# A decoder layer's feed-forward: a first tile pair of plain products, another order on GpSimd, another product order, and four token tiles at the end

## The chip, the cores and the metric

One core of one Trainium2 chip runs the whole kernel. The metric is the device time of one execution in microseconds (us). The engines are TensorE (PE in the profile, with its weight loads as PEld), VectorE (DVE), ScalarE (ACT), GpSimd (POOL) and SyncE (SP), which issues nearly all the DMAs.

## What is computed

The layer has an RWKV-7 group and an attention group, whose outputs are mixed, added to the input and normalised. A feed-forward follows. The change touches only what comes after the mix product, in float32:

```python
x = layer_norm(ALPHA * x + mix, ln1_g[l], ln1_b[l])
f = jnp.square(jax.nn.relu(x @ w_ffn1[l])) @ w_ffn2[l]
x = layer_norm(ALPHA * x + f, ln2_g[l], ln2_b[l])
```

There are 1024 tokens, a model width of 1024 and a hidden width of 4096.

## The kernel before, in words

**Precision.** Each float32 operand is split into a high part (a copy to the format fp32r, mostly by ScalarE) and a low part (VectorE or GpSimd subtracts). Each product is three matmuls, high by high, high by low, and low by high. In all these products the moving operand has 512 columns; a transpose is a matmul with 128.

**Seven products for eight.** Both feed-forward products are cut into 2x2 blocks and done by a Strassen-Winograd scheme with seven block products, p1 to p7, instead of eight. A block product of the first half is 4 contraction tiles (`HK`) of 3 matmuls, 12 in all, and leaves one 128x512 bank. The scheme needs sums of the weight blocks (s1 to s4, GpSimd, function `sums`), sums of the token blocks (`b12_raw`, `t3_raw` and the t tiles, made once by VectorE and GpSimd), and sums of the results (VectorE, `added`).

**First half (FFN1).** The 4096 hidden rows are 32 tiles, taken as 16 pairs u = 0 to 15 (`NU`): tiles u and u+16. For each pair TensorE does seven products, so 84 matmuls. ScalarE and VectorE split the weight pieces of the next pair (`w_high`, `w_low`); GpSimd sums its weight blocks (`sums(u + 1)`) and forms four sums of the hidden tiles of the present pair (`hidden_sums(u)`), which the second half needs. VectorE combines the seven results (`added`) and applies relu and square (`squared`). SyncE writes seven tiles of each pair to DRAM (`spill`) and loads the weights two pairs ahead into one landing buffer (`load1`). All engines run the lists written here in program order and meet at semaphores.

In program order GpSimd does, for each pair, `sums(u+1)` and then `hidden_sums(u)`; `hidden_sums(0)` comes before the loop. On VectorE `w_low(nxt, 2)` stands between the p6 and p7 results, and p5's result waits until the sums of the pair before are made.

**The first pair (u = 0)** runs while the first normalisation ends. Its p1 and p2 use tokens 0 to 511 (`LO`), which are normalised and transposed early. Its other products need tokens 512 to 1023 (`HI`): TensorE transposes them (`turn_high`), and for each contraction tile ScalarE, VectorE and GpSimd form and split the token sums. There are two buffers each of `b12_raw` and `t3_raw`, and one bank each for B12 and B22.

**Second half (FFN2).** There are 56 steps q = 8 i + p: product i of seven, contraction pair p of eight. A step has 24 matmuls (2 contraction tiles, 4 token tiles, 3 terms). It needs a pair of hidden tiles from DRAM and a piece of `w_ffn2`, 512 KB each, loaded by `load2(q)` into one of six stages (`RING`), and split by `high2` and `low2`. For the products listed in `COMBINED` GpSimd subtracts a 128x1024 weight piece first (`combine`). When a product's eight steps are done, VectorE reads its four banks (`read`), and GpSimd adds kept parts (`add`); both stand three steps later in their engine's list (`LAG = 3`). The last four steps are run token tile by token tile. Each of the eight token tiles has statistics (`part_stats`, `aggregate`), and a `finish` of two 128x1024 operations on VectorE, then a DMA.

```python
for u in range(1, NU):
    if u < NU - 1:
        sums(u + 1)
    hidden_sums(u)
```

Of the kernel before, what the change touches and what calls it, by code (L numbers as in the profile page):

```python
# [24 lines left out]
P = 128  # L25
# [1913 lines left out]
def mix_ffn(nc, mem, k, t, out):  # L1939
# [28 lines left out]
    b12_raw = [mem.at(f"b12_raw{j}", 70 + 4 * j, [P, HALF]) for j in range(2)]  # L1968
    t3_raw = [mem.at(f"t3_raw{j}", 72 + 4 * j, [P, HALF]) for j in range(2)]
# [41 lines left out]
    first_set = pieces("0", (A12_, quarters(190, 0), 198, 190), (S12_, None, 178, 202),  # L2011
                       (("s3", "a22"), quarters(190, 1), 174, 194), (("s4",), None, 182, 4))
    second_set = pieces("1", (A12_, quarters(46, 0), 42, 38), (("s1",), None, 62, 188),
                        (("s2", "s4"), quarters(46, 0), 54, 46), (("s3", "a22"), quarters(46, 1), 58, 50))
# [6 lines left out]
    def raw_of(u, name):  # L2021
# [9 lines left out]
           for i, n in enumerate(("h11", "h12", "h21", "h22", "s1", "s2", "s3", "s4"))}  # L2031
    ORDER = ("p1", "p5", "p6", "p7", "p3", "p2", "p4")
    order = lambda u: {0: ("p1", "p2", "p3", "p7", "p5", "p6", "p4"),
                       1: ("p1", "p2", "p5", "p6", "p7", "p3", "p4")}.get(u, ORDER)
    FIRST_BANK = {"p1": 0, "p2": 0, "p3": 4, "p4": 1, "p5": 2, "p6": 3, "p7": 5}
    BANKS = (6, 7, 3, 5, 2, 4, 0, 1)
    READ = {"p1": 1, "p6": 1, "p7": 2, "p5": 4, "p3": 5, "p2": 6, "p4": 7}
    nth = lambda u, name: 7 * (u - 1) + order(u).index(name)
    bank_of = lambda u, name: FIRST_BANK[name] if u == 0 else BANKS[nth(u, name) % 8]
    B12_BANK, B22_BANK = 6, 7  # L2040
# [26 lines left out]
    PAIR_BANK = ((2, 4), (6, 0))  # L2067
    banks = lambda b, n: ps[:, b:b + n, :]

    with ExitStack() as ctx:  # L2070
# [25 lines left out]
        def _(sp):  # L2096
# [44 lines left out]
            sp.wait_ge(sums_w, 8)  # L2141
            for n in (1, 3):
                sp.wait_ge(t_split[n][1], T_ALL)
            sp.wait_ge(t2_made, T_ALL)
            for u in range(NU):
                if u < NU - 2:
                    if u:
                        sp.wait_ge(lo_w, 4 * (u + 1) + 2)
                        sp.wait_ge(sums_w, 4 * (u + 2))
                    load1(u + 2)  # L2150
                elif u == NU - 1:
                    sp.wait_ge(prod, 7 * (NU - 1))
                    sp.wait_ge(lo_w, 4 * NU)
                    sp.wait_ge(sums_w, 4 * NU)
# [28 lines left out]
        def _(pe):  # L2183
# [22 lines left out]
            def turn_high(kt):  # L2206
                if kt:
                    pe.wait_ge(b12_copied, kt)
                turn(B12_BANK, 4, kt).then_inc(b12_ready, 1)
                if kt:  # L2210
                    pe.wait_ge(b22_lo, kt)
                turn(B22_BANK, 4, HK + kt).then_inc(b22_ready, 1)
# [13 lines left out]
            def whole(u, name):  # L2226
                i, _ = wset(u)[1][STILL[name]]
                pe.wait_ge(lo_w, 4 * u + i + 1)
# [28 lines left out]
            turn_high(0)  # L2257
            pe.wait_ge(lo_w, 4)
# [579 lines left out]
```

## Time and profile before

| | us |
|---|---|
| median of 3 runs | 1521.74 |
| lowest and highest run | 1521.64, 1525.98 |
| the profiled execution: its own time | 1523.78 |
| the profiled execution: its span | 1522.0 |
| TensorE busy | 1406.6 (92%) |
| VectorE busy | 918.1 (60%) |
| ScalarE busy | 450.6 (30%) |
| GpSimd busy | 447.2 (29%) |
| mean granted TensorE clock | 0.961 |

A span runs from the first to the last instruction of one execution. The granted clock is a share of TensorE's full speed of 2.4 GHz, so 0.5 is 1.2 GHz. Busy times of matmuls are modelled and overlap, so stretches are better compared by the distance between starts than by busy time. A row's square bracket gives the idle time before it and what ended it.

### The profile page before, as it was taken

Reading aid. Unit: us, or ns where it says so; the run is one execution under the profiler, and the core shown is the slowest. Engines: PE = TensorE matmul, PEld = TensorE weight load, DVE = VectorE, ACT = ScalarE, POOL = GpSimd, SP = SyncE. Lnnn points to the kernel's source line nnn. Section 1 sums busy time; section 2 is a strip of 40 time slices with the busy share of each in tenths; the row PEclk is TensorE's granted clock in tenths of the full one; section 3 lists DMA queues with packets and bytes.
Section 4 is the critical chain, followed back from the end, with each engine's and each line's share of the span. In section 5 each row is a group of like instructions: output and inputs, shape, how many; then the busy total and the mean of one; then the engine's idle time right before and its main releaser. Section 6 shows DMA issues by size and latency. Waiting matters only on the chain. (4 is left out here: it accounts for less than half of the span.)

```text
span 1522.0 us, 24832 instructions
## 1 busy us (share of the span) xinstructions
PE 1406.6 (92%) x10596; PEld 1149.6 (76%) x10596; DVE 918.1 (60%) x1020; ACT 450.6 (30%) x614; POOL 447.2 (29%) x291
## 2 busy tenths in 40 slices
PE   6999999888999799999699699999998799999995
PEld 5878888666777599996588488777777588888874
DVE  3547654263655244436747977766665675757768
ACT  2134433133344333322103412222111344433320
POOL 0000223200242200000137565555564154411450
PEclk8999999989999899999899799999999899999998
DMA  5111244578358921111413134433434787555642
GB/s 199 42 56 50 90 147 145 151 158 234 87 152 252 222 66 44 44 25 56 171 65 110 42 125 153 147 143 127 150 145 152 269 276 249 193 193 194 194 138 111
DMA packets 144686, 211.80 MB, mean 139 GB/s; under 512 B 79456, under 2 KB 82144, under 8 KB 143936
## 3 DMA queue, kind: packets, MB, share of 16 engines
q1 hardware_dynamic: 144384, 209.69, 43.1%
q8 instruction: 84, 1.38, 0.4%
q10 hardware_dynamic: 192, 0.52, 0.1%
q14 instruction: 26, 0.21, 0.0%
HBM read 136.18 MB, written 64.29 MB: 132 GB/s over the span
## 5 line engine op out<-in xcount | busy, mean ns | idle before, releaser
L2288 PE MATMUL banks<-stage_b_hi,stage_a_hi 128*128 128x512 f32 x448 | 177.5, 396 | 18.9 <-DVE stage_b_lo L2520 11.9
L2288 PE MATMUL banks<-stage_b_lo,stage_a_hi 128*128 128x512 f32 x448 | 176.8, 395 | 0.0
L2288 PE MATMUL banks<-stage_b_hi,stage_a_lo 128*128 128x512 f32 x448 | 176.6, 394 | 0.0
L2517 DVE TENSOR_TENSOR stage_a_lo<-stage_a_raw,stage_a_hi 128x1024 fp32r<-128x1024 f32 x56 | 98.2, 1754 | 72.0 <-ACT stage_a_hi L2376 71.9
L2288 PEld LDWEIGHTS banks<-stage_b_hi,stage_a_hi 128*128 128x128 f32 x448 | 85.7, 191 | 39.0 <-DVE stage_b_lo L2520 13.6
L358 PE MATMUL banks<-xT_hi,win_hi 128*128 128x512 f32 x320 | 103.6, 406 | 4.6 <-DVE xT_lo L705 4.6
L358 PE MATMUL banks<-xT_lo,win_hi 128*128 128x512 f32 x320 | 100.4, 395 | 0.0
L358 PE MATMUL banks<-xT_hi,win_lo 128*128 128x512 f32 x320 | 100.1, 395 | 0.0
L2288 PEld LDWEIGHTS banks<-stage_b_lo,stage_a_hi 128*128 128x128 f32 x448 | 85.7, 191 | 18.0
L2288 PEld LDWEIGHTS banks<-stage_b_hi,stage_a_lo 128*128 128x128 f32 x448 | 85.5, 191 | 17.9
L2376 ACT ACTIVATE stage_a_hi<-stage_a_raw 128x1024 fp32r<-128x1024 f32 x56 | 59.3, 1058 | 132.5 <-DMA stage_b_raw<-in_w_ffn 108.2
L2683 POOL TENSOR_TENSOR tile_s<-tile_h,tile_h 128x512 f32<-128x512 f32 x32 | 41.4, 1294 | 142.9 <-DVE tile_h L2498 142.9
L1140 PE MATMUL banks<-probs,v_all 128*128 128x512 f32 (+3 forms) x192 | 75.0, 504 | 0.7 <-ACT probs L1235 0.7
L358 PEld LDWEIGHTS banks<-xT_hi,win_hi 128*128 128x128 f32 x320 | 60.8, 193 | 19.1 <-DVE xT_lo L705 4.8
L1301 DVE TENSOR_REDUCE row_max_parts<-banks 128x1 f32<-128x512 f32 (+1 forms) x96 | 50.1, 552 | 35.7 <-PE banks L1092 24.0
L358 PEld LDWEIGHTS banks<-xT_lo,win_hi 128*128 128x128 f32 x320 | 61.3, 191 | 13.2
L358 PEld LDWEIGHTS banks<-xT_hi,win_lo 128*128 128x128 f32 x320 | 61.2, 191 | 13.0
L1235 ACT ACTIVATE probs<-banks 128x1024 f32<-128x1024 f32 (+3 forms) x64 | 41.6, 651 | 88.7 <-PE banks L1125 51.4
L2498 DVE SCALAR_TENSOR_TENSOR tile_h<-tile_h 128x512 f32<-128x512 f32 x64 | 63.1, 986 | 1.7
L2702 POOL TENSOR_TENSOR w_slots<-stage_b_raw,w_slots 128x1024 f32<-128x1024 f32 x16 | 41.8, 2611 | 65.0 <-DMA stage_b_raw<-in_w_ffn 65.0
L747 POOL COPY norm_wide<-key_norm 128x1024 f32<-128x1024 f32 x4 | 5.1, 1264 | 186.5 <-DVE cum_tile L666 186.5
L1363 POOL TENSOR_TENSOR att_out<-att_v,att_sum 128x512 f32<-128x512 f32 x7 | 8.9, 1271 | 168.2 <-DVE att_sum L1315 139.6
(375 smaller groups left out, 3626.2 us busy)
## 6 DMA issues: line engine op xcount, KB each, us to landing
stage_b_raw<-in_w_ffn SPq DMA_DIRECT2D x50, 512.0 KB, 4.6
w_landed<-in_w_ffn SPq DMA_DIRECT2D x32, 512.0 KB, 4.4
hid_s<-tile_s SPq DMA_DIRECT2D x64, 256.0 KB, 2.0
stage_a_raw<-hid_s SPq DMA_DIRECT2D x32, 512.0 KB, 3.7
hid_h<-tile_h SPq DMA_DIRECT2D x48, 256.0 KB, 2.0
stage_a_raw<-hid_h SPq DMA_DIRECT2D x24, 512.0 KB, 3.7
win_raw<-in_w_in SPq DMA_DIRECT2D x20, 512.0 KB, 3.6
x_tok<-in_x SPq DMA_DIRECT2D x8, 512.0 KB, 7.4
```

Source lines behind the costliest of these rows:

```text
L358: last = mm(ps[:, 2 * j + b, :], w[j][:, kt, :], r[:, kt, b * HALF:(b + 1) * HALF], start=kt == 0 and i == 0, stop=kt == KT - 1 and i == 2)
L747: G.tensor_copy(out, src).then_inc(wide_done, 1)
L1140: last = mm(ps[:, O[b], lo - b * HALF:HALF], pair[:, 64 * (h % 2):64 * (h % 2) + P], probs[kt % 3][:, lo:(b + 1) * HALF], start=kt == 0, s ...
L1235: A_(probs[kt % 3][:, kt * P:S], flat(T[kt % 2])[:, kt * P:S], ACT.Exp, scale=SCALE)\
L1301: V.reduce_max(tops[:, n, qt:qt + 1], ps[:, b, 0:width], AX_X).then_inc(a_free[b], 1)
L1363: G.tensor_tensor(k.att_out[:], k.att_v[:], k.att_sum[:], ALU.mult).then_inc(y_ready, 1)
L2288: last = nc.tensor.matmul(ps[:, bank, :], s[a][:, j, tok], s[b][:, j, :], start=p == 0 and j == 0 and n == 0, stop=p == NP - 1 and j == 1 ...
L2376: A(s["a_hi"][:], s["a_raw"][:], COPY).then_inc(hi2, 1)
L2498: V.scalar_tensor_tensor(hid[name][:], hid[name][:], 0.0, hid[name][:], ALU.max, ALU.mult).then_inc(hid_done, 1)
L2517: V.tensor_tensor(s["a_lo"][:], s["a_raw"][:], s["a_hi"][:].bitcast(F32), ALU.subtract).then_inc(lo2, 1)
L2683: G.tensor_tensor(dst, a, b, op).then_inc(sums_h, 1)
L2702: G.tensor_tensor(dst, a, b, ALU.subtract).then_inc(combined, 1)
```

## The change

It has five parts.

1. **Pair 0** isn't done with seven products. Its four result tiles (h11, h21, h12, h22) are plain products of 8 contraction tiles by 3 matmuls, 96 matmuls, the two for tokens 0 to 511 first. ScalarE applies relu and VectorE the square. No weight sums are needed for it (`sums(0)` goes), only its two pieces of weights. The token sums aren't needed for it either: they now stand beside the plain products and beside pair 1, in whole buffers (`b12_raw`, `t3_raw` of four tiles) and with two banks each for the transposes. Pair 1 takes the order p1, p2, p3, p7, p5, p6, p4.
2. **GpSimd** does `sums(u + 1)` and then `hidden_sums(u - 1)`: the hidden sums stand one pair later. `sums(u)` waits for pair u-2, as before.
3. **VectorE and SyncE in FFN1**: `w_low(nxt, 3)` stands before p5. In the last pair the splits of steps 0 and 1 of FFN2 stand after p5 and after p2 instead of at the head; `load2(2)` and `load2(3)` are issued inside the last pair, and the last spills of pair 14 no longer stand ahead of pair 15's.
4. **FFN2's product order**: the one combined product among the last three (h22) comes fifth (i = 4) instead of seventh, and the last (h21) isn't combined. The token tiles 4 to 7 are complete after the fifth product. So their statistics and `finish` stand at steps 44 to 49, and only token tiles 0 to 3 are left for the end.
5. **The reads**: `read(3)` has two more 128x1024 operations (the base of tiles 0 to 3), `read(4)` is now a plain addition for tiles 4 to 7, and `add(4)` of GpSimd goes; its four additions stand in `add(5)`.

The core of the diff ("..." marks what is left out):

```diff
-    A_OF = ("h11", "s1", "s2", "s3", "s4", "h21", "h22")
-    B_OF = ((0, 0), (0, 1), (1, 1), (0, 0), (1, 1), (1, 0), (1, 0))
-    COMBINED = (1, 2, 3, 6)
+    A_OF = ("h11", "s1", "s2", "s3", "h22", "s4", "h21")
+    B_OF = ((0, 0), (0, 1), (1, 1), (0, 0), (1, 0), (1, 1), (1, 0))
+    COMBINED = (1, 2, 3, 4)
...
-    PAIR_BANK = ((2, 4), (6, 0))
+    STATS_AT = (44, 45, 46, 47)
+    LAST_TILES = (4, 5, 6, 7, 0, 1, 2, 3)
+    PAIR_BANK = ((6, 0), (2, 4))
...
+            sp.wait_ge(sums_w, 4)
+            sp.wait_ge(t_split[1][1], T_ALL)
+            load1(2)
+            spill(0, ("h22", hid_done, 1), ("h11", hid_done, 3), ("h21", hid_done, 4))
+            for u in range(1, NU):
...
+                    sp.wait_ge(lo_w, split_base(u + 1) + 2)
+                    sp.wait_ge(sums_w, 4 * (u + 1))
                     load1(u + 2)
...
+                if u == NU - 1:
+                    sp.wait_ge(prod, 7 * (NU - 2))
+                    sp.wait_ge(lo_w, split_base(NU))
+                    sp.wait_ge(sums_w, 4 * (NU - 1))
                     load2(0)
                     load2(1)
-                spill(u)
-            sp.wait_ge(prod, 7 * NU)
-            for q in range(2, STEPS):
+                    sp.wait_ge(prod, prods(u, "p5"))
+                    load2(2)
+                spill(u - 1, *SUMS)
...
+                if u == NU - 1:
+                    sp.wait_ge(prod, prods(u, "p2"))
+                    load2(3)
+                spill(u, ("h21", hid_done, 4))
+            spill(NU - 1, *SUMS)
+            sp.wait_ge(prod, 7 * (NU - 1))
+            for q in range(4, STEPS):
...
+            pe.wait_ge(lo_w, 2)
+            pe.wait_ge(xlow_hi, HK + 2)
+            for part in range(2):
+                pe.wait_ge(xlow_lo, HK * (part + 1))
+                for i in range(2):
+                    for kt in range(HK * part, HK * (part + 1)):
+                        last = first(i, kt, x_hi[:, kt, LO], x_lo[:, kt, LO], i)
+                    if part:
+                        last.then_inc(first_mm, 1)
...
+            for kt in range(2):
+                turn_high(kt)
+            for kt in range(HK):
+                pe.wait_ge(b12_lo, kt + 1)
+                pe.wait_ge(b22_lo, kt + 1)
+                for i in range(2):
+                    for n, part in enumerate((kt, HK + kt)):
...
+                if kt + 2 < HK:
+                    turn_high(kt + 2)
...
             second_half(0)
+            second_half(1)
+            first_part(0)
+            first_part(1)
+            second_half(2)
+            second_half(3)
             for kt in range(HK):
                 high_t(3, kt)
-                if kt < HK - 1:
-                    second_half(kt + 1)
-                for n in (1, 2, 4):
-                    high_t(n, kt)
             act.wait_ge(x1_out, 16 * TT)
-            act.wait_ge(sums_w, 8)
+            act.wait_ge(sums_w, 4)
             for i in (1, 2, 3):
                 w_high(1, i)
+            for kt in range(HK):
+                high_t(1, kt)
+                high_t(2, kt)
+            first_part(2)
+            first_part(3)
+            for kt in range(HK):
+                high_t(4, kt)
...
+                    for q in range(4):
+                        high2(q)
...
+                dve.wait_ge(b12_hi, kt + 1)
+                V.tensor_tensor(t_lo[4][:, kt, :], b12_raw[:, kt, :], t_hi[4][:, kt, :].bitcast(F32), ALU.subtract)\
+                    .then_inc(b12_lo, 1)
                 dve.wait_ge(b22_hi, kt + 1)
-                V.tensor_tensor(t3_raw[kt % 2][:], ps[:, B22_BANK, :], b12_raw[kt % 2][:], ALU.subtract).then_inc(t3_made, 1)
-                V.tensor_tensor(x_lo[:, HK + kt, HI], ps[:, B22_BANK, :], x_hi[:, HK + kt, HI].bitcast(F32), ALU.subtract)\
+                V.tensor_tensor(x_lo[:, HK + kt, HI], ps[:, b22_bank(kt), :], x_hi[:, HK + kt, HI].bitcast(F32), ALU.subtract)\
                     .then_inc(b22_lo, 1)
+                V.tensor_tensor(t3_raw[:, kt, :], ps[:, b22_bank(kt), :], b12_raw[:, kt, :], ALU.subtract).then_inc(t3_made, 1)
...
+                second_half(kt)
             for i in (1, 2, 3):
                 w_low(1, i)
+            for kt in range(HK):
+                for n in (3, 1, 2):
+                    low_t(n, kt)
+            dve.wait_ge(first_mm, 4)
+            for kt in range(HK):
+                low_t(4, kt)
...
-                if 0 < u < NU - 1:
+                if nxt < NU:
                     w_low(nxt, 0)
                     w_low(nxt, 1)
-                elif u:
-                    low2(0, 0)
...
-                if 0 < u < NU - 1:
+                if nxt < NU:
                     w_low(nxt, 2)
                 settle(u, 1)
                 added(u, "p7", u3_sb[:], u2_sb[:])
+                if nxt < NU:
+                    w_low(nxt, 3)
                 settle(u, 2)
                 dve.wait_ge(sums_h, 4 * u)
-                left(u, "h22")
...
-                if 0 < u < NU - 1:
-                    w_low(nxt, 3)
-                elif u:
-                    low2(1, 0)
-                    low2(1, 1)
+                if nxt == NU:
+                    low2(0, 0)
+                    low2(0, 1)
...
+                if nxt == NU:
+                    low2(1, 0)
+                    low2(1, 1)
...
+                    for h in range(2):
+                        at = xo[:, 2 * h:2 * h + 2, LO]
+                        V.scalar_tensor_tensor(at, at, ALPHA, p1_all[:, 2 * h:2 * h + 2, :], ALU.mult, ALU.add).then_inc(based, 1)
+                elif i == 4:
+                    dve.wait_ge(based, 6)
+                    for h in range(2):
+                        at = xo[:, 4 + 2 * h:6 + 2 * h, LO]
+                        V.tensor_tensor(at, banks(bank[h], 2), at, ALU.add).then_inc(read2, 1)
...
+                if q in STATS_AT:
+                    tt = LAST_TILES[STATS_AT.index(q)]
...
+                    dve.wait_ge(read2, 6)
+                    part_stats(tt, 0)
+                    part_stats(tt, 1)
+                    aggregate(tt)
+                if q - 2 in STATS_AT:
+                    finish(LAST_TILES[STATS_AT.index(q - 2)], (slice(0, D),))
+            dve.wait_ge(added2, 6)
+            for tt in range(4):
...
+                dve.wait_ge(out_mm, tt + 1)
+                step.mark(V.tensor_tensor(xo[:, tt, LO], ps[:, PAIR_BANK[0][tt // 2] + tt % 2, :], xo[:, tt, LO], ALU.add))
...
-            sums(0)
...
+            for kt in range(HK):
                 pool.wait_ge(t2_made, kt + 1)
-                G.tensor_tensor(b21, b21, b11, ALU.subtract).then_inc(t4_made, 1)
+                G.tensor_tensor(xt_raw[:, HK + kt, :], xt_raw[:, HK + kt, :], xt_raw[:, kt, :], ALU.subtract).then_inc(t4_made, 1)
...
-            hidden_sums(0)
             for u in range(1, NU):
                 if u < NU - 1:
                     sums(u + 1)
-                hidden_sums(u)
+                hidden_sums(u - 1)
+            hidden_sums(NU - 1)
...
-                dst, a, b = {1: (at, s, at), 2: (at, s, at), 3: (s, at, s), 6: (s, s, at)}[i]
+                dst, a, b = {1: (at, s, at), 2: (at, s, at), 3: (s, at, s), 4: (s, s, at)}[i]
...
-                first, cut, kept, ready = {
-                    3: (4, HI, (p5_all,), (based, 0)), 4: (0, HI, (u2_all, p5_all), (read2, 4)), 5: (0, LO, (p1_all,), (read2, 6))}[i]
+                first, kept, ready = {3: (4, (p5_all,), (based, 0)), 5: (0, (u2_all, p5_all), (read2, 6))}[i]
...
-                if (q - LAG) % NP == NP - 1 and 3 <= (q - LAG) // NP < 6:
+                if (q - LAG) % NP == NP - 1 and (q - LAG) // NP in (3, 5):
```

## Rows read from the trace of the kernel before

**Rows 1.** windows; columns: stretch, its us, then busy us of each engine (instructions), PEclk, DMA
```profile
832.90:876.90 44.00, 30.47 (x117) 22.92 (x116) 40.51 (x42) 20.43 (x33) 23.46 (x16) 0.77 0.19 70
876.90:1175.90 299.00, 288.42 (x1261) 235.47 (x1259) 207.26 (x218) 58.65 (x70) 169.38 (x116) 1.00 0.39 142
1175.90:1211.30 35.40, 21.66 (x74) 17.01 (x74) 22.30 (x23) 12.51 (x13) 5.39 (x4) 0.81 0.68 254
1211.30:1477.70 266.40, 266.40 (x1177) 220.60 (x1176) 179.28 (x110) 105.24 (x103) 108.81 (x40) 1.00 0.65 214
1477.70:1507.30 29.60, 24.46 (x97) 18.77 (x96) 28.43 (x40) 2.83 (x7) 0.28 (x1) 0.94 0.22 87
1507.30:1522.00 14.70, 0.01 (x1) 0.00 (x0) 11.25 (x17) 0.59 (x2) 0.00 (x0) 0.66 0.28 112
```

**Rows 2.** timeline of the SP queue; columns: start, duration, instruction
```profile
1194.07 0.38 SPq L2120 DMA_DIRECT2D stage_a_raw<-hid_h  x1
...
1456.19 0.33 SPq L2120 DMA_DIRECT2D stage_a_raw<-hid_h  x1
...
1461.63 0.33 SPq L2120 DMA_DIRECT2D stage_a_raw<-hid_h  x1
```

**Rows 3.** timeline of TensorE before and in pair 0 (L2197 transposes)
```profile
825.80 1.80 PE L2197 MATMUL banks<-ident,x 128*128 128x128 f32 x15
...
862.66 0.80 PE L2222 MATMUL banks<-x1T_hi,w_hi 128*128 128x512 f32 x1 [4.47 <-DVE x1T_lo L2477]
```

**Rows 4.** timeline of all engines around pair 15's start (brackets: idle time before)
```profile
1151.13 1.74 POOL L2645 TENSOR_TENSOR wo_raw<-w_landed 128x512 f32<-128x512 f32 x1
...
1157.00 2.00 ACT L2319 ACTIVATE wo_hi<-wo_raw 128x1024 fp32r<-128x1024 f32 x2 [11.30 <-POOL wo_raw L2653]
...
1159.46 0.47 PE L2222 MATMUL banks<-x1T_hi,wo_hi 128*128 128x512 f32 x1 [1.07 <-DVE wo_lo L2424]
...
1164.38 1.29 POOL L2683 TENSOR_TENSOR tile_s<-tile_h,tile_h 128x512 f32<-128x512 f32 x1 [7.42 <-DVE tile_h L2498]
```

**Rows 5.** timeline of all engines, end of pair 15
```profile
1176.89 1.06 ACT L2376 ACTIVATE stage_a_hi<-stage_a_raw 128x1024 fp32r<-128x1024 f32 x1 [17.89 <-DMA stage_b_raw<-in_w_ffn]
...
1180.26 0.68 DVE L2503 TENSOR_TENSOR u_sb<-banks,p_sb 128x512 f32<-128x512 f32 x1
...
1183.05 0.79 PE L2288 MATMUL banks<-stage_b_hi,stage_a_hi 128*128 128x512 f32 x1 [6.98 <-DVE tile_h L2503]
```

**Rows 6.** waits of TensorE, 1184 to 1507 us: total, times, longest
```profile
PE banks L2288 <- DVE stage_b_lo L2520: 11.9, 4, 6.8
```

**Rows 7.** timeline of VectorE in and after pair 0
```profile
840.20 1.28 DVE L2467 SCALAR_TENSOR_TENSOR x<-x,ln_sd,ln_bias 128x1024 f32<-128x1024 f32 x1
...
855.06 0.68 DVE L2477 TENSOR_TENSOR x1T_lo<-banks,x1T_hi 128x512 fp32r<-128x512 f32 x1
...
857.37 3.43 DVE L2484 TENSOR_TENSOR t_lo<-x1T_raw,t_hi 128x512 fp32r<-128x512 f32 x2
...
868.40 1.28 DVE L2484 TENSOR_TENSOR t_lo<-x1T_raw,t_hi 128x512 fp32r<-128x512 f32 x2
...
882.93 4.01 DVE L2424 TENSOR_TENSOR we_lo<-w_landed,we_hi 128x1024 fp32r<-128x1024 f32 x2
```

**Rows 8.** timeline of VectorE in FFN2
```profile
1369.15 2.35 DVE L2575 TENSOR_TENSOR u_all<-banks,u_all 128x1024 f32<-128x1024 f32 x2 [7.99 <-PE banks L2288]
1371.61 9.03 DVE L2581 SCALAR_TENSOR_TENSOR x_out<-x_out,u_all 128x1024 f32<-128x1024 f32 x4
...
1420.72 3.41 DVE L2517 TENSOR_TENSOR stage_a_lo<-stage_a_raw,stage_a_hi 128x1024 fp32r<-128x1024 f32 x1
```

**Rows 9.** timeline of GpSimd in FFN2
```profile
1372.92 6.64 POOL L2713 TENSOR_TENSOR x_out<-x_out,p_all 128x1024 f32<-128x1024 f32 x2 [28.67 <-DVE x_out L2581]
```

**Rows 10.** timeline of VectorE at the end
```profile
1509.89 0.68 DVE L2628 TENSOR_TENSOR x_out<-banks,x_out 128x512 f32<-128x512 f32 x1
...
1514.49 0.69 DVE L2628 TENSOR_TENSOR x_out<-banks,x_out 128x512 f32<-128x512 f32 x1
```

More of the change, by code:

```diff
@@ L1967, in mix_ffn @@
     xt_raw = mem.at("x1T_raw", 78, [P, KT, HALF])
-    b12_raw = [mem.at(f"b12_raw{j}", 70 + 4 * j, [P, HALF]) for j in range(2)]
-    t3_raw = [mem.at(f"t3_raw{j}", 72 + 4 * j, [P, HALF]) for j in range(2)]
+    b12_raw = mem.at("b12_raw", 70, [P, HK, HALF])
+    t3_raw = mem.at("t3_raw", 150, [P, HK, HALF])
     t_hi = {n: mem.at(f"t{n}_hi", 126 + 16 * (n - 2), [P, HK, HALF], F32R) for n in (2, 3, 4)}
@@ L2206, in turn_high, with first @@
             def turn_high(kt):
[L2207 to L2212, printed above, removed]
+                if kt >= 2:
+                    pe.wait_ge(b12_hi, kt - 1)
+                    pe.wait_ge(t3_made, kt - 1)
+                turn(b12_bank(kt), 4, kt).then_inc(b12_ready, 1)
+                turn(b22_bank(kt), 4, HK + kt).then_inc(b22_ready, 1)
+            def first(i, kt, b_hi, b_lo, bank):
+                made, _ = first_set
+                _, a_hi, a_lo = made[i]
+                j, cut = kt // HK, slice(kt % HK * P, (kt % HK + 1) * P)
+                for n, (a, b) in enumerate(((a_hi, b_hi), (a_hi, b_lo), (a_lo, b_hi))):
+                    last = nc.tensor.matmul(ps[:, bank, :], a[:, j, cut], b, start=kt == 0 and n == 0,
+                                            stop=kt == KT - 1 and n == 2)
+                return last
             def one(u, name, kt):
@@ L2256, in _ @@
             pe.wait_ge(last_normed, 1)
-            turn_high(0)
-            pe.wait_ge(lo_w, 4)
-            for name, ready in (("p3", b22_lo), ("p7", t_split[3][1]), ("p5", t_split[1][1]), ("p6", t_split[2][1]),
-                                ("p4", t_split[4][1])):
-                for kt in range(HK):
-                    if name == "p3" and kt < HK - 1:
-                        turn_high(kt + 1)
-                    pe.wait_ge(ready, kt + 1)
-                    last = one(0, name, kt)
-                last.then_inc(prod, 1)
+            for kt in range(2):
[5 more added lines that the diff above has]
+                    for n, part in enumerate((kt, HK + kt)):
+                        b_hi, b_lo = (t_hi[4][:, kt, :], t_lo[4][:, kt, :]) if n == 0 else (x_hi[:, part, HI], x_lo[:, part, HI])
+                        made, _ = first_set
+                        _, a_hi, a_lo = made[i]
+                        cut = slice(kt * P, (kt + 1) * P)
+                        for m, (a, b) in enumerate(((a_hi, b_hi), (a_hi, b_lo), (a_lo, b_hi))):
+                            last = nc.tensor.matmul(ps[:, 2 + i, :], a[:, n, cut], b, start=kt == 0 and n == 0 and m == 0,
+                                                    stop=kt == HK - 1 and n == 1 and m == 2)
+                    if kt == HK - 1:
+                        last.then_inc(first_mm, 1)
+                if kt + 2 < HK:
+                    turn_high(kt + 2)
+            BUILT = {"p7": t_split[3][1], "p5": t_split[1][1], "p6": t_split[2][1], "p4": t_split[4][1]}
             for u in range(1, NU):
@@ L2405, in keep @@
                     A(dst[:, 2 * h:2 * h + 2, :], banks(PAIR_BANK[i][h], 2), COPY).then_inc(copied2, 1)
-            for q in range(2, STEPS):
+            roots = 0
+            for q in range(4, STEPS):
                 high2(q)
@@ L2410, in _ @@
                     keep((q - LAG) // NP)
[L2411 to L2413 removed]
+                if q - 1 in STATS_AT:
+                    root2(LAST_TILES[roots])
+                    roots += 1
+            for tt in LAST_TILES[4:]:
+                root2(tt)
         @block.vector
```

215 lines of the change are left out of this document (88 added, 127 removed).

## Prediction

> **What bounds the kernel now.** I read four views in this order: the windows by stage, the waits of TensorE, the timelines where TensorE stands still, and the timelines of the engines it waits for. The reader is to see that TensorE is the bound from 832.9 us on, but with gaps, and that after its last matmul 14.7 us follow without it [rows 1]. The stages before 832.9 us are left alone.
>
> A step of FFN2 takes 1461.63 - 1456.19 = 5.44 us when nothing is late [rows 2]. That is 24 matmuls, so 0.2267 us each. With this price the stages of [rows 1] come apart:
>
> - Pair 0 takes 44.0 us. Its 84 matmuls are worth 19.0 us and its 32 transposes, at 1.80/15 = 0.12 us [rows 3], 3.8 us. The rest is waiting for token sums, one gap of 4.47 us among it, at the lower clock level in part (granted clock 0.77).
> - Pairs 1 to 15 take 299.0 us, and 15 x 84 matmuls are worth 285.6 us. The missing 13.4 us are a bubble of about 1.3 us at the p5 product of each later pair, until VectorE has split the sums of weights [rows 4]. What sets it is a loop: GpSimd's weight sums start at 1151.13, ScalarE begins to split them at 1157.00, VectorE follows and only then takes p7 and p5, and after these GpSimd gets its hidden tiles at 1164.38, with the next weight sums behind them [rows 4].
> - FFN2, from 1175.9 to 1507.3, takes 331.4 us, and 56 steps are worth 304.6 us. Of the missing 26.8 us, 7.0 [rows 5] and 11.9 [rows 6] are idle. The other 7.9 us are matmuls at the lower clock level (1.2 GHz) after the gaps of 7.0, 6.8 and 3.4 us (granted clock 0.81 and 0.94 in [rows 1]): some 2.5 us for each long gap.
>
> **Pair 0.** It gets 96 matmuls, 21.8 us, and keeps 32 transposes, 3.8 us. The first 48 matmuls need only tokens 0 to 511 and last 10.9 us, to 843.8; the last normalisation ended at 840.20 + 1.28 [rows 7], so it is hidden. Then 16 transposes. The first B22 tile is ready after three copies of ScalarE (about 0.5 us each, half of one of 128x1024 in [rows 4]) and two operations of VectorE from PSUM of 0.68 us [rows 7], some 1.1 us after the transposes. Later tiles are hidden behind 12 matmuls each, but for about 0.4 us. Sum: 21.8 + 3.8 + 1.5 = 27.1 us, a gain of **16.9**. Bounds: 25.6 without waits, 31 if the clock falls at this gap. I take it not to fall, as the bubbles of 1.07 us [rows 4] leave the clock at 1.00 [rows 1].
>
> **Pairs 1 and 2.** Pair 1 starts at 860.0 and asks for p7 after three products, at 868.2. For that VectorE must have split the third sum of all four tiles. Its list: last `t3_raw` at about 858.2, then three weight splits, then 12 `low_t` of which the tenth is the one wanted. GpSimd meanwhile makes six sums, to about 868.5. With GpSimd at work a VectorE subtraction of 128x512 takes 3.43/2 = 1.7 us and one of 128x1024 takes 4.01/2 = 2.0 us; alone the small one takes 0.64 us [rows 7]. So 2.0 + 2.0 + 3 x 1.7 brings it to 867.3 to 868.5 with two `low_t` done, and eight more take 4.8 us: 873.3. TensorE waits 5.1 us, and 2.5 us for the clock. Pair 2 starts at 860.0 + 19.0 + 7.6 = 886.6.
>
> Pair 2's p6 goes to the bank of pair 1's p2, so it waits for VectorE to have taken that. The chain: ten more operations of VectorE (two `low_t`, four of t4, four squares) to 879.3; `sums(2)`, which now waits for these squares, 5.9 us (1151.13 to 1157.00 [rows 4]) and some 0.8 of contention, to 886.0; `hidden_sums(0)`, four of 1.29 us [rows 4] with waits of their own, 6.2 us, to 892.2; VectorE's wait for these stands ahead of p5, and six operations of 0.68 us end with p2 at 896.3. TensorE is there at 892.0: 4.3 us and 2.5 us for the clock, 6.8 us. Bounds for both stalls together: 8 us if VectorE is never held up by GpSimd (then only the second chain is late), 20 us if every step is contended. I take 7.6 + 6.8 = 14.4.
>
> **Pairs 3 to 15.** `sums(u + 1)` can start when pair u starts and ends at +5.9; the splits are done by about +13, and the next pair wants them at +19. `hidden_sums(u - 1)` ends at +12.1, when VectorE has just taken p7 and split its weights. So the loop is gone, and a pair is 84 matmuls, 19.04 us. The queue behind VectorE's wait for the hidden sums is p5, p3, p2, p4; the next pair asks for the p5 bank only at +24.5. `load1` and the spills move in SP's queue: a load is issued at +6 and has 13 us. FFN1 after pair 0: 285.6 + 14.4 = 300.0 us against 299.0, a loss of **1.0**: the bubbles pay for the two stalls.
>
> **Into FFN2.** Before, the splits of step 0 stood ahead of pair 15's results in VectorE's list and their load ended at 1176.89, so the p6 result was taken at 1180.26 and TensorE waited 6.98 us for a bank [rows 5]. Step 2 was loaded at 1194.07 [rows 2], after all spills. Now the splits stand behind p5 and p2, at +13 and +18 of the pair, with the load ended at about +7; `load2(2)` goes out at +6 and `load2(3)` at +18, and step 2 is wanted at +30. Both gaps go. If this cover failed, each would cost its 7 us and 2.5 us again.
>
> **Step 35.** `read(3)` starts at step 32 and took 2.35 and then 9.03 us for four operations, two of them held up by GpSimd's two additions of 6.64 us [rows 8, 9]. One VectorE operation beside one of GpSimd costs about 3.35 us (3.41 in [rows 8]). It ended 11.6 us after the step's start; step 35 is wanted at 16.3. Now two more operations stand there, and then the two splits of step 35. And GpSimd, which had nothing to combine in the fifth product, now has `combine(35)` to `combine(38)` behind its additions. Taking turns, VectorE ends at 11.6 + 4 x 3.35 = 25.0. TensorE waits 8.7 us and loses 2.5 us by the clock: 11.2 us. The lower bound is nothing: alone such an operation takes (9.03 - 6.64)/2 = 1.2 us, and 11.6 + 4 x 1.2 = 16.4. I take the full price, since the rows show turns whenever both have work.
>
> **Last steps.** Statistics and finishes of four tiles (about 4 us each) move into steps 42 to 49: with splits of 2.35 us and the read that is 37 us of VectorE in 43.5 us, and it runs ahead (idle 7.99 us at step 32 [rows 8]). GpSimd's four additions now hold up the splits of steps 51 and 52 only; those of 53 to 55 end about 23 us after step 48 starts, and are wanted from 23.1 to 25.8. So the gaps behind 1477.7 go. FFN2: 304.6 + 11.2 = 315.8 us against 331.4, a gain of **15.6**.
>
> **End.** VectorE needs 4.6 us for a tile (1509.89 to 1514.49 [rows 10]), TensorE 5.44 us for its quarter of the last four steps. With nothing left from other tiles VectorE keeps up, and after the last matmul there remain 0.2 us and the 7.5 us from 1514.49 to the span's end: 7.7 against 14.7, a gain of **7.0**.
>
> **Sum.** 16.9 - 1.0 + 15.6 + 7.0 = 38.5 us off the span of 1522.0: 1483.5. The profiled execution took 1523.78 us itself, 2.0 above the median of the runs, 1521.74; taken off the median it gives 1483.2 us.
>
> **Rivals.**
>
> - *No wait at step 35.* If VectorE gets its operations through, TensorE never stops there: 1483.2 - 11.2 = 1472. For it speaks that it is a matter of 8.7 us in eight operations; against it the turns of [rows 8, 9]. Chance 0.25. The Trainium skill (SBUF — State Buffer, section "SBUF: two separate sides") has VectorE and GpSimd share one port pair under an exclusive lock held for a whole instruction by whoever starts first; it promises no turns, so VectorE could win several times running, and the time would be 1472; with turns it stays 1483. It exempts operations that read PSUM, and the 0.68 us one amid GpSimd's work [rows 7] agrees.
> - *The loop stays*, because something else in VectorE's list is late each pair: 13 pairs at 20.3 us cost 17 us more, 1500. Chance 0.08. Against it: 5 us to spare in each pair.
> - *The loads into FFN2 aren't hidden*: 9.5 to 19 us more, 1493 to 1502. Chance 0.07.
> - *Still fewer stalls* in pairs 1 and 2 beside none at step 35: under 1465. Chance 0.07.
> - *Slower than before.* The hidden sums come too late: VectorE can't free the p5 bank. It starts when GpSimd's eight sums end later than 24.5 - 1.4 = 23.1 us after the pair's start; slower overall needs 14 pairs at 19.04 + 38.5/14 = 21.8 us, so an end at 25.9 in place of 12.1. The longest sum in [rows 4] is 1.74 us, and eight of those are 13.9. Chance 0.03.
>
> **Chances and range.** The forecast has 0.5, by itself 1476 to 1491. To hold 8 in 10 the range takes in the first rival and the upper bounds of the stalls: 1465 to 1494. A difference under 0.3%, 4.6 us, can't be told from none: slower 0.03 (the last rival), same 0.03 (the loop and the loads going wrong together, with the full stalls), faster 0.94.
>
> **What would show it.** Pair 0 some 27 us long; one gap before p7 of pair 1 and one before p6 of pair 2; no bubbles from pair 3 on; no gap between the halves; a gap at step 35, with VectorE's operations of 3.3 us beside `combine`; no gaps in the last four steps, and 7.7 us after the last matmul. It would be wrong above all if contention of VectorE and GpSimd is milder or harsher than in these rows.

## Result, and the profile after

The changed kernel takes 1486.5 us (median of 4 runs, 1485.18 to 1489.19), the kernel before beside it 1521.93 us (1521.64 to 1525.98). The ratio is 0.976, 95% interval 0.974 to 0.979: 35.4 us less, where 38.5 were predicted. The profiled execution took 1487.25 us with a span of 1485.5.

First the windows of the changed kernel by stage, with the columns of [rows 1]: pair 0, pairs 1 and 2 up to the end of their stalls, the other pairs, FFN2, and what follows the last matmul.

```profile
832.90:860.20 27.30, 25.66 (x129) 21.16 (x128) 15.80 (x21) 12.30 (x22) 15.70 (x12) 1.00 0.18 73
860.20:906.00 45.80, 34.08 (x133) 27.04 (x133) 37.79 (x41) 16.31 (x26) 32.24 (x20) 0.85 0.29 104
906.00:1161.80 255.80, 255.80 (x1131) 211.87 (x1130) 191.50 (x204) 56.94 (x67) 169.61 (x103) 1.00 0.46 161
1161.80:1477.70 315.90, 307.40 (x1345) 253.87 (x1343) 239.44 (x173) 113.82 (x117) 114.09 (x41) 0.98 0.63 211
1477.70:1485.50 7.80, 0.22 (x1) 0.00 (x0) 4.57 (x8) 0.29 (x1) 0.00 (x0) 0.80 0.34 134
```

From 906.0 to 1161.8 TensorE is busy for 255.80 of 255.80 us: the bubble of each pair [rows 4] is gone. As long as TensorE has work, the granted clock is below 1.00 only in the two stretches with waits of over 5 us, pairs 1 and 2 and one place of FFN2. Next all waits of TensorE from 832 to 1490 us (total, times, longest).

```profile
PE banks L2321 <- DVE stage_b_lo L2564: 8.5, 1, 8.5
PE banks L2243 <- DVE tile_h L2551: 5.9, 1, 5.9
PE banks L2243 <- DVE t_lo L2531: 5.3, 1, 5.3
PE banks L2293 <- DVE x1T_lo L2521: 1.6, 2, 1.3
PE banks L2243 <- DVE we_lo L2472: 0.4, 1, 0.4
```

Six gaps are left. The timeline of TensorE says where (the matmul behind a gap, and of some its successors; the gap of 0.4 us, at p5 of pair 2, isn't shown).

```profile
843.63 1.91 PE L2209 MATMUL banks<-ident,x 128*128 128x128 f32 x16
846.82 0.47 PE L2293 MATMUL banks<-t_hi,w_hi 128*128 128x512 f32 x1 [1.28 <-DVE x1T_lo L2521]
847.13 0.39 PE L2293 MATMUL banks<-t_lo,w_hi 128*128 128x512 f32 x1
...
857.40 0.47 PE L2293 MATMUL banks<-t_hi,w_hi 128*128 128x512 f32 x1 [0.35 <-DVE x1T_lo L2521]
...
873.91 0.80 PE L2243 MATMUL banks<-t_hi,w_hi 128*128 128x512 f32 x1 [5.35 <-DVE t_lo L2531]
874.50 0.63 PE L2243 MATMUL banks<-t_lo,w_hi 128*128 128x512 f32 x1
874.93 0.63 PE L2243 MATMUL banks<-t_hi,w_lo 128*128 128x512 f32 x1
...
899.15 0.79 PE L2243 MATMUL banks<-t_hi,we_hi 128*128 128x512 f32 x1 [5.95 <-DVE tile_h L2551]
...
1360.81 0.80 PE L2321 MATMUL banks<-stage_b_hi,stage_a_hi 128*128 128x512 f32 x1 [8.50 <-DVE stage_b_lo L2564]
1361.40 0.63 PE L2321 MATMUL banks<-stage_b_lo,stage_a_hi 128*128 128x512 f32 x1
```

The gaps of 5 us and more stand before p7 of pair 1, p6 of pair 2 and step 35, as forecast. Behind them matmuls come 0.43 us apart (874.50 to 874.93), the lower clock level; behind the gap of 1.28 us they come 0.23 us apart once the first two have started, the upper one. FFN2's start follows from step 35: 1360.81 - 8.50 - 35 x 5.44 = 1161.9.

VectorE and, below it, GpSimd from step 32 on (compare [rows 8, 9]):

```profile
1336.03 2.36 DVE L2624 TENSOR_TENSOR u_all<-banks,u_all 128x1024 f32<-128x1024 f32 x2 [6.47 <-PE banks L2321]
1338.49 9.03 DVE L2630 SCALAR_TENSOR_TENSOR x_out<-x_out,u_all 128x1024 f32<-128x1024 f32 x4
1347.44 6.73 DVE L2633 SCALAR_TENSOR_TENSOR x_out<-x_out,p_all 128x1024 f32<-128x1024 f32 x2
1354.10 3.37 DVE L2561 TENSOR_TENSOR stage_a_lo<-stage_a_raw,stage_a_hi 128x1024 fp32r<-128x1024 f32 x1
1357.39 3.37 DVE L2564 TENSOR_TENSOR stage_b_lo<-stage_b_raw,stage_b_hi 128x1024 fp32r<-128x1024 f32 x1
...
1339.79 6.64 POOL L2768 TENSOR_TENSOR x_out<-x_out,p_all 128x1024 f32<-128x1024 f32 x2 [12.59 <-DVE x_out L2630]
1346.39 16.60 POOL L2758 TENSOR_TENSOR stage_b_raw<-stage_b_raw,w_slots 128x1024 f32<-128x1024 f32 x5
```

From 1347.44 VectorE's four operations take 6.73/2, 6.73/2, 3.37 and 3.37 us, and GpSimd's five take 16.60/5 = 3.32 us each: from here to GpSimd's last `combine` they take turns without an exception.

VectorE at the end (compare [rows 10]):

```profile
1461.63 0.69 DVE L2681 TENSOR_TENSOR x_out<-banks,x_out 128x512 f32<-128x512 f32 x1 [3.21 <-PE banks L2321]
...
1477.95 0.69 DVE L2681 TENSOR_TENSOR x_out<-banks,x_out 128x512 f32<-128x512 f32 x1 [0.75 <-PE banks L2321]
```

Here it is VectorE that waits for TensorE, 0.75 us at the last tile, and 7.55 us follow. Before, VectorE lagged: its last tile came 7.2 us after TensorE's end at 1507.3.

### The profile page after: what moved, and what is told of

Same layout as the page of the kernel before. It is cut to its first block, busy times and chain, and to the rows that moved or that the text cites. A ratio compares the mean times of both kernels' runs of the same rounds, so it can differ in the third digit from the quotient of the medians.

```text
span 1485.5 us, 24855 instructions
## 1 busy us (share of the span) xinstructions
PE 1393.8 (94%) x10608; PEld 1145.3 (77%) x10608; DVE 919.2 (62%) x1017; ACT 450.6 (30%) x619; POOL 466.2 (31%) x285
## 4 chain that ended last, share of the span: by engine, by line
PE 45%; DVE 3%; issue 1%; POOL 1%; DMA 0%; ACT 0%; SPq 0%; DVEq 0%; POOLq 0%
PE banks L2321 20%; PE banks L2243 18%; PE banks L2202 6%; PE banks L2231 1%; DVE x_out L2630 1%; DVE x_out L2633 0%; DMA w_landed<-in_w_ffn 0%; PE banks L2293 0%; PE banks L2209 0%; DVE t_lo L2531 0%; DVE stage_b_lo L2564 0%; DVE stage_a_lo L2561 0%; DVE x1T_lo L2531 0%; POOL tile_s L2739 0%; DVE u_all L2624 0%
## 5 line engine op out<-in xcount | busy, mean ns | idle before, releaser
L2561 DVE TENSOR_TENSOR stage_a_lo<-stage_a_raw,stage_a_hi 128x1024 fp32r<-128x1024 f32 x56 | 102.0, 1822 | 42.7 <-ACT stage_a_hi L2414 42.7
L1301 DVE TENSOR_REDUCE row_max_parts<-banks 128x1 f32<-128x512 f32 (+1 forms) x96 | 50.1, 551 | 35.4 <-PE banks L1092 23.6
L358 PEld LDWEIGHTS banks<-xT_lo,win_hi 128*128 128x128 f32 x320 | 61.2, 191 | 13.1
L1796 POOL TENSOR_TENSOR k_undecayed<-hT,undecay 128x256 f32<-128x256 f32 x16 | 11.8, 740 | 134.9 <-ACT undecay L1657 134.9
L2564 DVE TENSOR_TENSOR stage_b_lo<-stage_b_raw,stage_b_hi 128x1024 fp32r<-128x1024 f32 x34 | 51.2, 1507 | 0.4
```

What stands on the lines that cost most here:

```text
L358: last = mm(ps[:, 2 * j + b, :], w[j][:, kt, :], r[:, kt, b * HALF:(b + 1) * HALF], start=kt == 0 and i == 0, stop=kt == KT - 1 and i == 2)
L1301: V.reduce_max(tops[:, n, qt:qt + 1], ps[:, b, 0:width], AX_X).then_inc(a_free[b], 1)
L2561: V.tensor_tensor(s["a_lo"][:], s["a_raw"][:], s["a_hi"][:].bitcast(F32), ALU.subtract).then_inc(lo2, 1)
L2564: V.tensor_tensor(s["b_lo"][:], src, s["b_hi"][:].bitcast(F32), ALU.subtract).then_inc(lo2, 1)
```

## Experiments

All kernels are the changed one with one edit more, and all were timed beside the kernel before. The stages ahead of the feed-forward, which no edit touches, vary by some 5 us from one execution to the next (the first transpose of pair 0's second half starts at 841.6 to 846.9). And the kernel before took 1521.9 us beside the changed kernel, 1525.6 beside e1 to e4, 1524.6 beside e5 to e8 and 1524.5 beside e9 and e10, so medians of different rows can be compared to some 4 us only. So the traces are also compared **from that transpose to the span's end**: 1485.5 - 843.63 = 641.9 us in the changed kernel. The last column is this difference. It is from one execution each, and the clock behind a gap moves it by up to 1.5 us for each gap (last section).

| run | median, us | ratio to before (95%) | from the transpose, us | against the changed kernel |
|---|---|---|---|---|
| changed kernel | 1486.5 | 0.976 (0.974-0.979) | 641.9 | |
| e1_pool_old_order | 1502.2 | 0.985 (0.984-0.986) | 656.3 | +14.4 |
| e2_base_late | 1480.6 | 0.971 (0.969-0.973) | 634.9 | -7.0 |
| e3_add_late | 1477.7 | 0.969 (0.968-0.971) | 630.4 | -11.5 |
| e4_both_late | 1477.4 | 0.968 (0.967-0.970) | 630.9 | -11.0 |
| e5_t3_first | 1488.1 | 0.976 (0.974-0.977) | 641.4 | -0.5 |
| e6_loads_late | 1495.9 | 0.981 (0.979-0.983) | 650.7 | +8.8 |
| e7_finish_end | 1490.7 | 0.978 (0.976-0.980) | 646.1 | +4.2 |
| e8_fine_waits | 1483.8 | 0.973 (0.971-0.974) | 638.5 | -3.4 |
| e9_late_fine | 1473.7 | 0.967 (0.966-0.969) | 625.4 | -16.5 |
| e10_best | 1473.0 | 0.967 (0.964-0.969) | 625.3 | -16.6 |

**e1_pool_old_order: does GpSimd's order remove the bubbles?**

```diff
             for u in range(1, NU):
+                hidden_sums(u - 1)
                 if u < NU - 1:
                     sums(u + 1)
-                hidden_sums(u - 1)
```

GpSimd's sequence is then that of the kernel before.

> The changed kernel, but GpSimd does the hidden sums of pair u-1 ahead of the weight sums of pair u+1 again. Theory: the old loop is back, so TensorE shows a bubble of about 1.3 us at p5 of each of some 12 later pairs and a pair takes 20.3 us in place of 19.04; 15 to 17 us more, less up to 6 us because the wait of pair 2 is another one: a span of 1495 to 1503 us. Rival: the bubbles went because VectorE's third weight split stands ahead of p5 and because the loads of weights are issued elsewhere; then the span stays within 3 us of 1485.5.

The waits of TensorE in this run, and two neighbouring p5 products:

```profile
PE banks L2243 <- DVE we_lo L2472: 8.3, 6, 4.4
...
PE banks L2243 <- DVE wo_lo L2472: 4.5, 6, 0.8
```

```profile
1115.95 0.47 PE L2243 MATMUL banks<-x1T_hi,wo_hi 128*128 128x512 f32 x1 [0.75 <-DVE wo_lo L2472]
1136.18 0.47 PE L2243 MATMUL banks<-x1T_hi,we_hi 128*128 128x512 f32 x1 [0.76 <-DVE we_lo L2472]
```

The bubbles are back, and a pair takes 1136.18 - 1115.95 = 20.23 us in place of 19.04. The trace has eleven of them, in pairs 5 to 15, which make 13.1 us. FFN2's first steps lose 2.9 us besides (2.1 of it in waits), and pair 2 and step 35 cost some 1.5 us less (in pair 2 the wait of 5.95 us at p6 turns into one of 4.4 at p5). By the traces the run is 14.4 us longer; by the medians, each against the kernel before beside it, 12.1. So one moved call is worth a third to two fifths of the whole gain of 35.4. The bubble is the loop described in the prediction, and pair 0 has no part in it.

**e2, e3, e4: which work makes step 35 late?** VectorE's two operations on tiles 0 to 3 (the base) go from step 32 to step 40 in e2; GpSimd's additions go behind step 39 and step 50's `combine` in e3; e4 has both.

```diff
 # e2
-                    for h in range(2):
-                        at = xo[:, 2 * h:2 * h + 2, LO]
-                        V.scalar_tensor_tensor(at, at, ALPHA, ...)
...
+                if q == 40:
+                    (the same three lines)
 # e3
-                if (q - LAG) % NP == NP - 1 and (q - LAG) // NP in (3, 5):
-                    add((q - LAG) // NP)
+                if q in (39, 50):
+                    add({39: 3, 50: 5}[q])
```

> The changed kernel, but the two additional base operations of read(3) stand on VectorE after step 40's splits. Theory (turns with GpSimd, 3.35 us for each operation of VectorE while GpSimd has work): step 35 is ready 18.3 us after the start of step 32 in place of 25.0, so TensorE waits 2.0 us in place of 8.5 and its clock doesn't fall: 8.9 us less, a span near 1476.6. Rival (VectorE's own list is too long, GpSimd has no part in it): two operations at their own 1.2 us, 2.3 us less, 1483.

> The changed kernel, but GpSimd's two additions after the fourth product stand behind combine(39) instead of behind combine(34). VectorE's list is unchanged. Theory: GpSimd then has only combine(37) and combine(38) in this stretch, as their loads land, so two of VectorE's eight operations are held up and step 35 is ready about 16 us after the start of step 32, when it is wanted at 16.3: the gap of 8.5 us and the clock's 2.4 us go, a span near 1475. Rival (VectorE's list alone): no change, 1485.5.

> Both moves together: the two base operations after step 40, the two additions behind combine(39). Theory: no gap at step 35 with 7 us to spare, but nothing more to win than with the additions alone: a span near 1474.5. If the two causes add up in another way than by turns, this one is clearly faster than either alone.

In e3 and e4 no gap is left at step 35. VectorE in e4, then GpSimd:

```profile
1347.04 1.21 DVE L2561 TENSOR_TENSOR stage_a_lo<-stage_a_raw,stage_a_hi 128x1024 fp32r<-128x1024 f32 x1
...
1349.31 3.42 DVE L2561 TENSOR_TENSOR stage_a_lo<-stage_a_raw,stage_a_hi 128x1024 fp32r<-128x1024 f32 x1
...
1348.76 2.88 POOL L2759 TENSOR_TENSOR stage_b_raw<-stage_b_raw,w_slots 128x1024 f32<-128x1024 f32 x1 [2.73 <-DMA stage_b_raw<-in_w_ffn]
```

A split costs 1.21 us while GpSimd is idle and 3.42 beside a `combine`. It ends 1.09 us after the `combine` does (1352.73 and 1351.64), which is about its own time alone. So it stood still until then, and the two didn't share a port at part speed. The gain of 11 us is the whole price that the prediction set on this place (8.7 + 2.5): in the changed kernel the gap and the slow matmuls behind it took 11.3. Moving GpSimd's additions is enough by itself; with the base alone moved away a small gap stays.

```profile
1355.96 0.71 PE L2321 MATMUL banks<-stage_b_hi,stage_a_hi 128*128 128x512 f32 x1 [1.92 <-DVE stage_b_lo L2564]
1356.46 0.63 PE L2321 MATMUL banks<-stage_b_lo,stage_a_hi 128*128 128x512 f32 x1
1356.89 0.63 PE L2321 MATMUL banks<-stage_b_hi,stage_a_lo 128*128 128x512 f32 x1
```

This is e2. Its gap is as expected, but behind it the matmuls come 0.43 us apart until 1359.45, some 1.7 us lost that weren't expected.

**e5_t3_first: is p7's wait in pair 1 only VectorE's order?** The four splits that p7 wants go ahead of the third weight piece and of the other token sums.

```diff
-            for i in (1, 2, 3):
-                w_low(1, i)
+            w_low(1, 1)
+            w_low(1, 2)
             for kt in range(HK):
-                for n in (3, 1, 2):
+                low_t(3, kt)
+            w_low(1, 3)
+            for n in (1, 2):
+                for kt in range(HK):
                     low_t(n, kt)
```

> The changed kernel, but on VectorE the splits of the third token sum stand ahead of the last weight split and of those of the first and second token sums. Theory: p7 of pair 1 waits 1.2 to 1.5 us in place of 5.3 and its clock stays up, but TensorE only comes earlier to the second gap, whose chain (load of pair 2's weights, weight sums, hidden sums, VectorE) starts just 1.5 us earlier: the wait before p6 of pair 2 grows from 5.9 to about 10.8 us, and the time falls by 1 to 2 us. Rival (the two gaps are independent prices, as the sum of the prediction has them): 6.4 us less.

```profile
869.88 0.50 PE L2243 MATMUL banks<-t_hi,w_hi 128*128 128x512 f32 x1 [1.12 <-DVE t_lo L2531]
...
882.81 0.47 PE L2243 MATMUL banks<-x1T_hi,we_hi 128*128 128x512 f32 x1 [1.47 <-DVE we_lo L2472]
...
889.34 0.47 PE L2243 MATMUL banks<-x1T_hi,we_hi 128*128 128x512 f32 x1 [3.53 <-DVE we_lo L2472]
...
898.27 0.80 PE L2243 MATMUL banks<-t_hi,we_hi 128*128 128x512 f32 x1 [4.62 <-DVE tile_h L2554]
```

p7 waits 1.12 us in place of 5.35, and p1, p5 and p6 of pair 2 wait for what p7 no longer waits for. Nothing is gained: p6 of pair 2 starts 54.5 us after the transpose (898.27 - 843.80), as in e2, e4, e6 and e7, which keep the old order. Pair 2 is bound by a chain that doesn't pass through p7.

**e6_loads_late: do the early loads hide the start of FFN2?** `load2(2)` and `load2(3)` go back behind the spills.

```diff
-                    sp.wait_ge(prod, prods(u, "p5"))
-                    load2(2)
...
-                if u == NU - 1:
-                    sp.wait_ge(prod, prods(u, "p2"))
-                    load2(3)
...
-            for q in range(4, STEPS):
+            for q in range(2, STEPS):
```

> The changed kernel, but the loads of steps 2 and 3 of the second half are issued behind all spills of pair 15 again. Theory: they go out about 8 us after pair 15 ends, step 2 is ready some 18 us after it and wanted at 10.9, so TensorE waits 7.2 us and loses 2.4 us by the clock: 9.6 us more, a span near 1495. Rival: with the splits of steps 0 and 1 out of the way these loads are hidden anyway; no change.

```profile
1178.67 0.79 PE L2316 MATMUL banks<-stage_b_hi,stage_a_hi 128*128 128x512 f32 x1 [6.08 <-DVE stage_b_lo L2559]
```

Step 2 waits 6.08 us and runs at the lower clock, which takes 8.5 us together. The other 0.3 us of the +8.8 have nothing to do with the edit: p6 of pair 2 started 1.0 us earlier than in the changed kernel, and the matmuls behind it lost 1.4 us more.

**e7_finish_end: what are early finishes worth?** The four finishes of tiles 4 to 7 go from steps 46 to 49 to behind the last step.

```diff
-                if q - 2 in STATS_AT:
-                    finish(LAST_TILES[STATS_AT.index(q - 2)], (slice(0, D),))
+            for tt in LAST_TILES[:4]:
+                finish(tt, (slice(0, D),))
```

> The changed kernel, but the finishes of token tiles 4 to 7 (four times 2.6 us of VectorE) stand behind the last split instead of at steps 46 to 49. Theory: VectorE idles 5.5 us in the last stretch (3.2 and three times 0.75), so of the 10.3 us 4.8 come out at the end: a span near 1490.3. Rival: the moved work costs as much as in the kernel before, where 7 us were lost behind the last matmul.

It cost 4.2 us: of the 7 us gained at the end more than half hangs on these eight operations. TensorE's waits are those of the changed kernel, and its last matmul ends 0.2 us sooner after the transpose. The loss is behind it: VectorE no longer waits for TensorE, and takes its last tile 4.7 us after TensorE's last matmul, which ends at 1475.5. In the changed kernel that was 0.2 us, in the kernel before 7.2.

```profile
1480.17 0.68 DVE L2681 TENSOR_TENSOR x_out<-banks,x_out 128x512 f32<-128x512 f32 x1
```

**e8_fine_waits: is the end of pair 2's chain GpSimd's four hidden sums?** VectorE waits for each of them where it overwrites what that one read, in place of all four before p5.

```diff
-                dve.wait_ge(sums_h, 4 * u)
+                dve.wait_ge(sums_h, 4 * u - 3)
...
+                dve.wait_ge(sums_h, 4 * u - 2)
...
+                dve.wait_ge(sums_h, 4 * u - 1)
...
+                dve.wait_ge(sums_h, 4 * u)
```

> The changed kernel, but VectorE waits for each hidden sum of the pair before only where it overwrites a tile that this sum reads (s1 before h22, s3 before h12, s2 before h11, s4 before h21) instead of for all four ahead of p5. Theory: in pair 1 VectorE starts p5 when its weight split ends, about 2.6 us before the last hidden sum, so p6 of pair 2 starts about 2.5 us earlier (a wait of 3.4 in place of 5.9 us); 2.5 us less, nothing in later pairs, a span near 1483. Rival: something else than the hidden sums holds this chain; no change.

```profile
897.80 0.79 PE L2243 MATMUL banks<-t_hi,we_hi 128*128 128x512 f32 x1 [2.83 <-DVE tile_h L2551]
```

The wait at p6 of pair 2 fell from 5.95 to 2.83 us (released by the same operation, one that writes `tile_h`), and the time by 3.4. Of this 2.7 us are the edit: p6 starts 51.8 us after the transpose here, as in e9 and e10, against 54.5 in e2, e4, e6 and e7. The changed kernel's own trace has 55.5, because a load was late in it (next section). So the hidden sums do stand in the chain; what is left of it lies ahead of them.

**e9_late_fine and e10_best: do the gains add?** e9 is e4 with e8; e10 is e9 with e5.

> The changed kernel with three of the changes tried singly so far put together: both additions at steps 32 to 34 moved later (worth about 11 us together, and leaving no gap at step 35) and the four finer waits on the hidden sums (worth about 3 us at the p6 product of pair 2). If the two stalls are independent, as the chain read from the traces has it, the gains add: p6 of pair 2 waits about 2.8 us, step 35 doesn't wait, and the time is about 1473.5 us median, between 1471 and 1476. Rival: the finer waits move work of VectorE or spills so that something is late elsewhere in the first half; then the time stays at that of the late additions alone, 1477 us.

> The one before, and in addition VectorE splits the third token sum's four tiles ahead of the third weight piece and of the other token sums. By itself that moved the wait from p7 of pair 1 (5.4 to 1.1 us) onto three later products of pair 2 and gained nothing, as the chain of the hidden sums ends at the same time. With the finer waits that chain is shorter at its end by 3 us, so part of what is moved should now be gained: p6 of pair 2 below 2.8 us, and 0 to 3 us less than the one before, about 1472 us. Rival: the chain's earlier part (VectorE's splits of the weights for pair 2) sets all of it, and the time is the same within 0.5 us, with gaps at p1 and p5 of pair 2.

They add: e9 is 16.5 us below the changed kernel, 3.3% below the kernel before, where 11.0 and 3.4 were to be added. p6 of pair 2 starts at 51.8 as in e8, and step 35 doesn't wait, as in e4. The surplus of 2.1 us isn't owed to the edits but to the clock: behind pair 2's gap the matmuls lost 2.9 us in e4 and 1.7 in e8, and next to nothing in e9, where the clock stayed up:

```profile
894.29 0.50 PE L2243 MATMUL banks<-t_hi,we_hi 128*128 128x512 f32 x1 [3.22 <-DVE tile_h L2551]
894.63 0.40 PE L2243 MATMUL banks<-t_lo,we_hi 128*128 128x512 f32 x1
894.87 0.39 PE L2243 MATMUL banks<-t_hi,we_lo 128*128 128x512 f32 x1
```

In e10 the four gaps are 1.1, 1.5, 3.6 and 1.8 us, 7.9 in all against 8.6 in e9, and the time from the transpose is 625.3 against 625.4. What e5 moves isn't gained here either.

## Why the prediction was right, and where it was off

**By stage.** The forecast had 27.1, 300.0, 315.8 and 7.7 us, 650.6 in all. Measured are 27.5 (832.74 to 860.24), 301.6, 315.9 and 7.8, 652.8, from a start that was 0.2 earlier. The span is 2.0 above the 1483.5 forecast. The median is 3.3 above its forecast: these 2.0, and 1.3 because this profiled execution was 0.75 us above its median, where I had taken off 2.0. No stage is off by more than 1.6 us. Within FFN1 two errors cancel in part, and that was luck: the waits of pairs 1 and 2 took 11.7 us in place of 9.4, and the lower clock behind them 3.6 in place of 5.0.

**Pair 0** was right in its parts: a gap of 1.28 us after the first transposes (forecast 1.1), 0.35 at the last tile, nothing at the clock. No run puts the seven products back, so that pair 0 gives 16.5 of the 35.4 us is read from the length of the stage (44.0 and 27.5).

**p7 of pair 1**: 5.35 us for 5.1, with the lower clock behind it. e5 confirms VectorE's order as its cause.

**p6 of pair 2** is the term that was sized too small: 5.95 us and 0.4 at p5, for 4.3. The step that was off is the chain's end at 896.3; it was 899.1. The chain as the trace has it, SP, GpSimd and VectorE in that order:

```profile
874.53 0.81 SPq L2109 DMA_DIRECT2D w_landed<-in_w_ffn  x2
...
881.12 1.29 POOL L2700 TENSOR_TENSOR we_raw<-w_landed 128x512 f32<-128x512 f32 x1 [12.63 <-DMA w_landed<-in_w_ffn]
...
893.59 1.26 POOL L2739 TENSOR_TENSOR tile_s<-tile_h,tile_s 128x512 f32<-128x512 f32 x1
...
877.50 2.50 DVE L2571 TENSOR_TENSOR tile_h<-first_relu 128x512 f32<-128x512 f32 x4
...
894.94 1.29 DVE L2551 TENSOR_TENSOR tile_h<-banks,u_sb 128x512 f32<-128x512 f32 x2 [2.64 <-issue]
...
898.42 0.68 DVE L2551 TENSOR_TENSOR tile_h<-banks,p_sb 128x512 f32<-128x512 f32 x1
```

The four squares ended at 880.0 (forecast 879.3). GpSimd then waited 1.1 us more, for the weights of pair 2, issued at 874.53; the prediction left that load out. Its four weight sums took 6.6 us (to 887.7), as forecast, and the four hidden sums 7.2 in place of 6.2. That makes 0.7 + 1.1 + 1.0 = 2.8 us, and TensorE came 1.2 later itself. The 1.1 us of the load belong to this execution and not to the kernel: the load is issued 3.0 us before the squares start in e2, e4, e6 and e7 as well, but there GpSimd waits for the squares alone, and p6 of pair 2 starts 54.5 us after the transpose in place of 55.5 (54.7 in e3). By the forecast it was 52.5 (896.3 - 843.8). So the lasting error is 2.0 us, from squares that end later and from hidden sums of 1.8 us each where 1.29 and some waiting was reckoned.

**Pairs 3 to 15** ran at 19.04 us without a bubble, and e1 shows that this is GpSimd's order.

**Step 35**: 8.50 us for 8.7. Against the rival of no wait, which had a chance of 0.25, stands that VectorE never ended two operations within one of GpSimd's there. The lock of the Trainium skill (SBUF — State Buffer, section "SBUF: two separate sides") fits the 3.3 us of an operation that takes 1.2 alone, and e4's split that stood still until GpSimd had ended. That neither engine gets it twice in a row when both want it is a thing that the rows show and the page doesn't promise. e3 and e4 turn the rival into a kernel: 1477.

**Into FFN2 and the end**: no gap; e6 and e7 give back 8.8 and 4.2 us. The new product order as such wasn't run the other way round, so its share of the 22.4 us gained in FFN2 and behind it (15.5 and 6.9) rests on the traces and on these two runs.

## What to carry to other kernels

If two engines share a port, count the operations that stand between an event and a deadline and price them all with turns, 3.3 us in place of 1.2 here. If it doesn't fit, move the work whose deadline is far off, on either engine. A bubble that returns in each iteration is a loop through several engines' lists, and the order of two calls on the least busy of them can be what holds it. When a wait is removed and nothing is gained, as in e5, look for the chain that ends at the next wait, and shorten that.

## What was not expected of the hardware

How long a gap is didn't decide what TensorE's clock did behind it. It stayed at the upper level after gaps of 1.28 us (pair 0), 1.81 (e10) and 3.22 (e9), and fell to the lower one, with matmuls 0.43 us apart, after gaps of 1.92 (e2) and 2.83 (e8). These are windows of about 4 us from the matmul behind the second gap of pair 2, of e9 and then of e8:

```profile
894.20:898.20 4.00, 3.90 (x17) 3.26 (x18) 3.93 (x5) 1.12 (x2) 3.82 (x3) 1.00 0.54 203
```

```profile
897.70:901.70 4.00, 3.90 (x10) 3.14 (x11) 3.93 (x5) 1.12 (x2) 3.80 (x3) 0.57 0.55 205
```

The two kernels have the same program at this place, and still it is 17 matmuls against 10, a granted clock of 1.00 against 0.57. In e10 a gap of 3.56 us was followed by five matmuls at full speed, and only then by the lower level.

```profile
889.63 0.47 PE L2243 MATMUL banks<-x1T_hi,we_hi 128*128 128x512 f32 x1 [3.56 <-DVE we_lo L2472]
```

What decides stays open. Nor is the price of a fall fixed. The forecast had 2.5 us for each; counted as the time from the first matmul behind the gap to the first at the usual distance, less 0.2267 us for each between, the changed kernel has 2.1 (ten matmuls, 873.91 to 878.27), 1.5 and 2.65. Behind the same gap of 5.4 us at p7 of pair 1, in the same program, it was 1.5 us in e4 and 3.0 in e6. All falls that ran their course cost 1.5 to 3.0 us, so a forecast carries 1.5 us of uncertainty for each long gap, and up to 3 us for a short one, where the clock may stay up.
